# Expert outputs summed into tokens by one-hot matmuls instead of read-add-write transfers, in a hybrid attention and sparse-expert block

## What is computed

```
logits = t @ w_router + b_router
top_val, top_idx = lax.top_k(logits, 4)
gate = softmax(top_val)
# for every expert e, over the tokens that chose it:
gu = xb @ w_gate_up[e] + b_gate_up[e]            # 1024 -> 2048
g, u = min(gu[:, :1024], 7), clip(gu[:, 1024:], -7, 7)
a = (u + 1) * (g * sigmoid(1.702 * g))
yb = a @ w_down[e] + b_down[e]                   # 1024 -> 1024
# x[token] += gate[token, e] * yb[row of that token]
```

## Time and profile before

| | |
|---|---|
| median of 3 runs | 1463.76 us (1462.33 to 1465.62) |
| the profiled execution | 1464.02 us |
| its span, first to last instruction | 1462.0 us |
| PE busy | 1342.6 us, 92% |
| DVE, ACT, POOL busy | 462.0, 270.6, 162.1 us |
| DMA over the span | 458.15 MB, 313 GB/s |
| mean granted PE clock | 0.985 |

### The profile page before, as it was taken

How to read it: one execution, slowest core, us unless ns; L and a number is a source line. 1 busy time by engine, 2 the same in 40 slices (tenths; PEclk the granted TensorE clock), 3 DMA queues, 4 the chain that set the end, 5 groups by cost and what they waited for, 6 DMA issues and landing times.

```text
span 1462.0 us, 26871 instructions
## 1 busy us (share of the span) xinstructions
PE 1342.6 (92%) x10905; PEld 656.5 (45%) x10905; DVE 462.0 (32%) x1112; ACT 270.6 (19%) x476; POOL 162.1 (11%) x247
## 2 busy tenths in 40 slices
PE   6999999999989999989898898989898898989986
PEld 5888878888933333323232232323233233323321
DVE  5113745665263232222222222232222223222211
ACT  4224535542221110011010000101000011110001
POOL 2001300000010111111010111111011111101111
PEclk9999999999999999999999999999999999999998
DMA  6332220013589999999999999999999999999993
GB/s 188 89 113 87 86 87 1 1 32 131 228 321 378 411 411 402 409 409 417 412 405 420 398 415 409 415 412 412 416 402 416 405 415 415 413 414 406 417 403 113
DMA packets 74614, 458.15 MB, mean 313 GB/s; under 512 B 10672, under 2 KB 28112, under 8 KB 41776
## 3 DMA queue, kind: packets, MB, share of 16 engines
q1 hardware_dynamic: 64544, 433.87, 72.9%
q0 software_dynamic: 9344, 21.37, 6.0%
q10 hardware_dynamic: 688, 2.38, 0.4%
HBM read 442.91 MB, written 14.68 MB: 313 GB/s over the span
## 4 chain that ended last, share of the span: by engine, by line
PE 70%; DMA 27%; ACT 1%; DVE 1%; issue 0%; POOL 0%; SPq 0%; ACTq 0%; DVEq 0%; POOLq 0%
PE ps L1659 28%; DMA gu_head<-in_w_gate_up_dram 13%; DMA gu_tail<-in_w_gate_up_dram 13%; PE ps L1698 9%; PE ps L1704 4%; PE ps L1371 3%; PE ps L1373 3%; PE ps L1372 3%; PE ps L1508 2%; PE ps L1395 2%; PE ps L1396 2%; PE ps L1397 2%; PE ps L1686 1%; PE ps L1362 1%; PE ps L1364 1%; PE ps L1363 1%
## 5 line engine op out<-in xcount | busy, mean ns | idle before, releaser
L1659 PE MATMUL ps<-gu_head,xT 128*32 128x512 f32 x3840 | 436.5, 607 | 72.7 <-DMA gu_head<-in_w_gate_up_dram 70.9
L1659 PEld LDWEIGHTS ps<-gu_head,xT 128*32 128x32 f32 x3840 | 122.5, 112 | 379.7 <-issue 271.7
L1186 DVE TENSOR_REDUCE row_f<-ps 128x2 f32<-128x4 f32 (+1 forms) x33 | 5.3, 161 | 513.1 <-PE ps L1623 513.1
L827 ACT COPY gu_tok<-ps 128x512 f32<-128x512 f32 x80 | 46.9, 586 | 607.8 <-PE ps L1659 607.8
L1659 PE MATMUL ps<-gu_tail,xT 128*32 128x512 f32 x1280 | 145.1, 599 | 11.0 <-DMA gu_tail<-in_w_gate_up_dram 11.0
L1698 PE MATMUL ps<-dn_even,aT 128*32 128x512 f32 x1024 | 122.0, 594 | 0.0
L1698 PE MATMUL ps<-dn_odd,aT 128*32 128x512 f32 x1024 | 113.2, 594 | 1.9 <-DVE y_b L1229 1.9
L617 POOL DMA_INDIRECT xg_a<-h_dram,idx_g x33 | 33.2, 1007 | 572.4 <-PE ps L1636 284.1
L880 DVE TENSOR_TENSOR st_l<-st_w,st_h 128x2048 fp32r<-128x2048 f32 x25 | 57.3, 2292 | 112.8 <-ACT st_h L689 112.8
L1659 PEld LDWEIGHTS ps<-gu_tail,xT 128*32 128x32 f32 x1280 | 41.0, 111 | 110.9 <-issue 84.8
L1222 DVE SCALAR_TENSOR_TENSOR aT<-act_u,act_g 128x768 f32<-128x768 f32 (+1 forms) x32 | 26.4, 825 | 158.6 <-PE ps L1704 119.3
(11 more groups left out here) (343 smaller groups left out, 1631.0 us busy)
## 6 DMA issues: line engine op xcount, KB each, us to landing
gu_head<-in_w_gate_up_dram SPq DMA_DIRECT2D x96, 2048.0 KB, 26.2
gu_tail<-in_w_gate_up_dram SPq DMA_DIRECT2D x32, 2048.0 KB, 26.9
dn_even<-in_w_down_dram SPq DMA_DIRECT2D x64, 1024.0 KB, 25.1
dn_odd<-in_w_down_dram SPq DMA_DIRECT2D x64, 1024.0 KB, 25.9
st_w<-in_w_in_dram SPq DMA_DIRECT2D x17, 1024.0 KB, 5.3
st_w<-in_w_out_dram SPq DMA_DIRECT2D x4, 1024.0 KB, 5.2
x_tok<-in_x_dram SPq DMA_DIRECT2D x4, 512.0 KB, 6.0
st_w<-in_w_o_swa_dram SPq DMA_DIRECT2D x4, 512.0 KB, 3.6
```

Of the source, the lines that this page charges most:

```text
L1659: ins = pe.matmul(ps[j * GROUP:(j + 1) * GROUP, n, :], xT[:, k, n * GROUP:(n + 1) * GROUP], gu_chunk(k)[:, j * 512:(j + 1) * 512], start=( ...
```

## The change

The output no longer receives additions by DMA. After `down(i)`, ACT writes the gated result as `y_hi` in fp32r and DVE (`keep_low`) what is missing to full precision as `y_lo`; both are 128 rows of 512: partitions 0 to 63 hold channels 0 to 511 of 64 slots, partitions 64 to 127 the other 512 channels. POOL builds one-hot tables (`put`): row of a slot, column of its token. In `gate_up(2)`, after every second channel block, PE multiplies table by rows (`pair_sums`): for a block `c` of 128 tokens 12 matmuls with 64 rows of contraction each, alternating between the upper and lower half of the array and between PSUM banks 6 and 7. DVE adds each block to the resident `x_tok` (`add_sums`), and PE's next block waits for that. `x_tok` is stored once at the end by SP. The rows gathered by POOL now come whole (one DMA per item, rows of 4 KB) and are turned by DVE in 32x32 blocks (`turn_rows`) and no longer by PE, except for item 0. After the loop, PE's order is down(30), gate_up(31), pair sums, turn_gate_up(31), down(31), sums of item 31.

```diff
-            def gather(small):
-                g.indirect_dma_start(out=xg_a[:, :], out_offset=None, in_=h2_rows[:, :],
-                                     in_offset=bass.IndirectOffsetOnAxis(ap=idx_g[:, 0:1], axis=0)).then_inc(xg_in, 16)
...
+            def gather(i):
+                n = 2 * GROUP if i % 2 else SLOTS
+                g.indirect_dma_start(out=xg[0:n, :], out_offset=None, in_=h2_dram[:, :],
+                                     in_offset=bass.IndirectOffsetOnAxis(ap=idx_g[0:n, 0:1], axis=0)).then_inc(xg_in, 16)
+            def put(table, n):
+                g.tensor_scalar(table[:, :], token_of[:, :], put_row[:, n:n + 1], None, ALU.is_equal).then_inc(put_ready, 1)
...
-                    gather(i % 2 == 1)
-                    add_rows(i - 1, pair)
+                gather(1)
+                pool.wait_ge(sums_ps, pair * 4 + 4)
...
+                put(put_odd, 0)
+                put(put_even, 1)
+                put(put_even_b, 2)
...
+                gather(2)
...
+                for a in (0,) if i % 2 else (0, 1):
+                    ins = sc.activation(y_hi[i % 2 * 2 + a][:, :], ps[:, 4 + a, :], ACT.Identity,
+                                        scale=gate_all[:, col, a:a + 1].rearrange("p a n -> p (a n)"))
+                ins.then_inc(y_high, 1)
...
+            def turn_rows(i, pair=None):
+                rows = slice(0, groups(i) * GROUP)
+                dve.wait_ge(xg_in, counted(32, 16 * i + 16, pair))
+                dve.wait_ge(bank_done, counted(5, groups_before(i), pair))
+                near = xg[:, :].rearrange("s (k p a) -> s p k a", p=P, a=2)
+                for n in range(groups(i)):
+                    s = slice(n * GROUP, (n + 1) * GROUP)
+                    for q in range(4):
+                        r = slice(q * GROUP, (q + 1) * GROUP)
+                        ins = v.transpose(xT[r, :, s].rearrange("r (k a) s -> r k a s", a=2),
+                                          near[s, r].rearrange("s p k a -> s k a p"))
+                ins.then_inc(x_raw, 1)
+                dve.wait_ge(x_raw, counted(2, i + 1, pair))
+                v.tensor_tensor(xT[:, :, rows], xT[:, :, rows], bc(g2_near[:, :], 2, groups(i) * GROUP), ALU.mult).then_inc(xT_ready, 1)
...
+            def keep_low(i, pair=None):
...
+                    ins = v.scalar_tensor_tensor(out=y_lo[n][:, :], in0=ps[:, 4 + a, :],
+                                                 scalar=gate_all[:, col, a:a + 1].rearrange("p a n -> p (a n)"),
+                                                 in1=y_hi[n][:, :].bitcast(F32), op0=ALU.mult, op1=ALU.subtract)
+                ins.then_inc(y_kept, 1)
+            def add_sums(c, n):
+                dve.wait_ge(sums_ps, n)
+                v.tensor_tensor(x_tok[:, c, :], x_tok[:, c, :], ps[:, 6:8, :].rearrange("p h n -> p (h n)"),
+                                ALU.add).then_inc(sums_added, 1)
...
+            def sums(parts, c, pair, n):
+                pe.wait_ge(sums_added, n)
+                for at, (table, y) in enumerate(parts):
+                    for half in (y_hi[y], y_lo[y]):
+                        for h in (0, 1):
+                            rows = slice(h * HD, (h + 1) * HD)
+                            ins = pe.matmul(ps[:, 6 + h, :], table[rows, c * P:(c + 1) * P], half[rows, :],
...
+                    if i == 2 and k % 2:
+                        pair_sums(k // 2, pair)
...
                     lists(i + 2, pair)
-                    turn_rows(i + 1, pair)
                     turn_gate_up(i, pair)
                     down(i - 1, pair)
+            down(0, n_pairs)
             gate_up(1, n_pairs)
+            for c in range(NB):
+                pair_sums(c, n_pairs)
             turn_gate_up(1, n_pairs)
-            down(0, n_pairs)
             down(1, n_pairs)
...
+            for c in range(NB):
+                sums(((put_odd, 2),), c, n_pairs, n_pairs * 4 + (c + 5)).then_inc(sums_ps, 1)
```

More of the change, by code:

```diff
@@ L307, in hybrid_block @@
         pairs_f = r2.put("pairs_f", [1, 1])
[L308 to L314, removed]
+        assert r2.at <= y_end
         r2.rewind(28 * K)
@@ L655, in _ @@
-            gather(False)
-            for c in range(NB):
-                pool.wait_ge(acc_set[c], 16)
+            pool.wait_ge(x_raw, 2)
+            gather(2)
             pool.wait_ge(items_ready, 1)
             n_pairs = pool.value_load(pairs[0:1, 0:1], min_val=PAIRS, max_val=MAX_PAIRS)
-            with pool.Fori(0, n_pairs) as pair:
-                for i in (1, 2):
-                    pool.wait_ge(idx_ready, pair * 2 + (i + 3))
-                    pool.wait_ge(xT_ps, pair * 2 + (i + 2))
-                    pool.sem_inc(turn, 1)
-                    gather(i % 2 == 1)
-                    add_rows(i - 1, pair)
@@ L667, in _ @@
[L667 to L668 removed]
+            pool.wait_ge(bdn_ps, 8)
+            g.memset(y_hi[2][:, :].bitcast(F32), 0.0)
+            then(g.memset(y_lo[2][:, :].bitcast(F32), 0.0))
+            g.tensor_copy(put_odd[:, :], y_lo[2][:, :].bitcast(F32)).then_inc(put_ready, 1)
+            then(g.tensor_copy(put_row[:, 1:3], row_all[:, 0, :]))
+            put(put_even, 1)
+            put(put_even_b, 2)
+            with pool.Fori(0, n_pairs) as pair:
+                pool.wait_ge(idx_ready, pair * 2 + 4)
+                pool.wait_ge(x_raw, pair * 2 + 3)
+                pool.sem_inc(turn, 1)
+                gather(1)
+                pool.wait_ge(sums_ps, pair * 4 + 4)
+                g.tensor_copy(put_row[:, 0:1], row_all[:, bass.ds(pair * 2 + 1, 1), 0:1].rearrange("p a n -> p (a n)"))
+                g.tensor_copy(put_row[:, 1:3], row_all[:, bass.ds(pair * 2 + 2, 1), :].rearrange("p a n -> p (a n)")).then_inc(row_copied, 1)
+                pool.wait_ge(row_copied, pair + 1)
+                pool.sem_inc(turn, 1)
+                put(put_odd, 0)
+                put(put_even, 1)
+                put(put_even_b, 2)
+                pool.wait_ge(idx_ready, pair * 2 + 5)
+                pool.wait_ge(x_raw, pair * 2 + 4)
+                pool.sem_inc(turn, 1)
+                gather(2)
@@ L1325, in _ @@
                     pick(i + 2, later, pair)
+                    if i == 2:
+                        for c in range(NB):
+                            add_sums(c, pair * 4 + (c + 1))
                     index(i + 2, pair)
                     keep_gates(i + 2, pair)
-                    move_rows(i + 1, pair)
+                    turn_rows(i + 1, pair)
                     activate(i, e, pair)
-                    if i == 1:
-                        weigh_odd(0, pair)
+                    keep_low(i - 1, pair)
+            keep_low(0, n_pairs)
+            for c in range(NB):
+                add_sums(c, n_pairs * 4 + (c + 1))
             e = dve.value_load(experts[0:1, bass.ds(n_pairs * 2 + 1, 1)], min_val=0, max_val=E - 1)
             activate(1, e, n_pairs)
-            weigh_odd(0, n_pairs)
+            keep_low(1, n_pairs)
+            for c in range(NB):
+                dve.wait_ge(sums_added, n_pairs * 4 + (c + 2))
+                add_sums(c, n_pairs * 4 + (c + 5))
         @block.tensor
```

216 lines of the change are left out of this document (98 added, 118 removed).

## The result

| | before | after |
|---|---|---|
| median, both kernels on one chip | 1464.3 us | 1483.9 us |
| ratio, 95% interval | 1 | 1.0127 [1.0112, 1.0142] |
| again, as run e1 | 1465.6 us | 1482.3 us, 1.0114 [1.0096, 1.0132] |
| span of the profiled execution | 1462.0 us | 1481.0 us (e1) |

The change makes the kernel 1.1 to 1.3% slower. I had forecast 1454 us, 0.7% faster; the result lies inside my range (1443 to 1492), on the other side of no change.

A forecast was written before the change was run, and what follows sets the result against it. DMA engines were taken to bound the steady state, with PE 12% behind. Start 489, loop 860 and end 103 gave a span of 1452 us, so 1454 against 1463.8, 0.7% faster; range 1443 to 1492.

The forecast's parts named there:

- the 2.6 to 3.6 that I gave: Loop: without the additions' packets, 3.6 us per pass, the DMA bound falls from 64.4 to 60.8 or 61.8 us.
- the price of a block transpose: DVE's turn of gathered rows: taken as 0.36 us per 256 elements, range 0.33 to 0.78; rival of slow transposes, chance 0.23.
- DVE "just in time" at T: Before gate_up(3): DVE's work after T ends at T + 8.3, PE wants to start at T + 8.8.
- I take 0.36: DVE's block transpose of 256 elements taken as 0.36 us each, since only the reading side steps.
- the pass of 61.4: Loop: 61.4 us per pass, from 61.1 for PE and 60.8 to 61.8 for DMA; before, 64.4.
- T + 8.8: When PE wants gate_up(3), after lists, 12 transposes (1.5 us) and down(1) (6.9 us).
- T + 8.5: When DVE is ready for gate_up(3), as the prediction's GpSimd tables rival states its own price.
- the 0.5 that I spoke of: Margin at T before gate_up(3) between DVE's readiness and PE's request: only 0.5 us.
- my own rule of 0.08 per 0.01 above 0.40: Before gate_up(3): from 0.40 us per transpose on, each 0.01 us more costs 0.08 us per pass.
- the rival that I had given 0.07: GpSimd's three tables stop DVE 0.7 us each behind T: pass 63.2 us, time 1479; chance 0.07.
- my 860: Loop: 14 intervals of 61.4 us make 860 us, where before stood 890.3.
- The gather moves the same bytes in one DMA per item and keeps the rest: DMA in the loop: whole-row gathers cost no more than before, so the additions' 3.6 us per pass is gained.

The follow-up runs named there:

- e1: The changed kernel run again unchanged, for a trace of an ordinary execution; 1482.3 us, 1.0114 against the kernel before.
- e3: The kernel before without its DMA additions to the output and the wait for them; 1415.3 us, 0.9662.
- e11: Changed kernel with fourth addition and tables late, PE turning item 1's rows, old tail order, half rows gathered onto 128 partitions, 128-element transposes; 1464.5 us.
- e5: The changed kernel with POOL's three tables built behind the gather of the next rows instead of ahead of it; 1478.4 us, 1.009.
- e4: The changed kernel with DVE's fourth addition of sums behind the activation of item 2 instead of ahead of its list; 1479.1 us, 1.0099.
- e14: e13 with the gather put back to whole rows of 4 KB on 64 or 96 partitions and block transposes of 256 elements; 1446.6 us.
- e13: e11 with DVE's gate operations behind the bias additions, separate PSUM banks in the tail, and y_lo left out of the sums; 1424.1 us.
- e8: The changed kernel with 26 unread matmuls of 512 columns in PE's gap ahead of the first gate_up(1); 1479.5 us, 1.0102.
- e2: The changed kernel with y_lo left out of the sums, 6 instead of 12 matmuls per block; 1469.2 us, 1.0028.

## Why the prediction was wrong

**Right.** Weights bound the kernel before, and the additions cost them about what I said: 2.95 us per pass (e3) against 3.6, inside the 2.6 to 3.6 that I gave. Their waits went. PE became the bound. A block of sums is 1.59 us, and the changes of form cost about 0.1 each. That the whole turned on the price of a block transpose, and at which place, was right as well: PE waits for DVE exactly before `gate_up(3)`, and nowhere else in the loop.

**The step that failed: DVE "just in time" at T, with "I take 0.36", and with it the pass of 61.4.** T, the end of the last block of sums in `gate_up(2)`, is 962.12 in e1. PE would have begun `gate_up(3)` at T + 8.9, and I had T + 8.8. DVE let it begin at T + 9.7, where my terms give T + 8.5 (the T + 8.3 was with 0.34 per transpose). So the margin was 0.3 us and not the 0.5 that I spoke of. Two terms were too small:

- The eight transposes take 3.61 us up to the product instead of 2.88, 0.73 more. A transpose is 0.448 us, because its fixed part is 0.18 us (e11), while I had priced it like an addition. The rule of the Trainium skill that I had weighed for it, 1.73 instead of 1.05 ns per column for a hopping source (Vector Engine (DVE) Microarchitecture Reference, Measured stream behaviour on trn2), doesn't show here: the slope is 1.03 ns per element. By my own rule of 0.08 per 0.01 above 0.40 this alone costs 0.4 us per pass, which isn't enough to turn the sign.
- The list and the gates take 2.04 us instead of 1.4, 0.64 more. This is the rival that I had given 0.07: GpSimd's tables hold up DVE, 0.69 us per pass by e5. A table takes 1.56 us, where I had 0.5 to 0.8, but it doesn't stop DVE for its whole length.

The other terms come out 0.14 below mine and PE 0.10 later: 0.73 + 0.64 - 0.14 - 0.10 - 0.32 of margin is the wait of 0.81. I had priced each rival alone, and the two add up. That the wait was DVE's is shown by e4, which takes it away, and e5, which leaves 0.12 us of it; no run has cheaper transposes, so their part is worked out from rows.

The rule that I had cited for the tables (the Trainium skill, SBUF — State Buffer, SBUF: two separate sides) names a second case beside two SBUF inputs, a DVE operation in a mode that uses two ports. The copy has one SBUF source, takes 0.62 instead of 0.17, and ends at 964.50, just when `put_odd` does (964.47), which agrees with an exclusion; which mode it ran in, no row shows. For a whole instruction the trace doesn't bear the exclusion out: both products of the gates have two SBUF inputs and end inside `put_even` (964.45 to 966.01, as far as POOL's rough times go).

PE's own rows were too small as well. Without the wait a pass takes 61.85 us (e4), where I had 61.1: blocks and the quarters of `gate_up(2)` around them are 0.50 above forecast, since each quarter after a block starts about 0.1 slower, and the two turns of `gate_up`, 1.61 and 1.33 instead of 1.53 and 1.16, 0.25. The wait and what is lost with it make the other 1.01, and the pass 62.86. Over 14 intervals this is 20 us above my 860: 14 from the wait, 6 from the 0.45 between 61.85 and my 61.4.

**"The gather moves the same bytes in one DMA per item and keeps the rest" was wrong too.** It costs all DMA traffic 1.8 us per pass, because the rows land on fewer partitions (63.1 us in e14 against 61.3 in e13). It is not in the result, since PE's 62.86 hid it, but it is why e4 and e5 gained 3 and 4 us only, and it would have taken the forecast's 61.4 up to 63.3 once the lead was used, in a kernel with a perfect DVE.

**The start, 5.6 us over.** The gap ahead of the first `gate_up(1)` grew from 1.88 to 6.11 us: DVE's turn lies in it, with eight transposes at 0.448. From the lists to `gate_up(1)` this is 3.7 us more, where I had added 3. That a gap of this length brings the lower clock, 2.5 us more, I had priced at the tail only (e8). `gate_up(0)` also begins 1.3 us later than before, where I expected it 1 us sooner. Its rows don't land sooner, and PE's gap ahead of them is 3.07 us instead of 2.04. The transposes of these rows and the stretch from there to `gate_up(0)`, first in the kernel before, then in e1:

```profile
426.19 0.74 PE L1633 MATMUL ps<-ident,xg_a 128*128 128x128 f32 x4 [2.04 <-DMA xg_b<-h_dram,idx_g]
426.19:428.89 2.70, 2.70 (x15) 1.61 (x15) 1.26 (x4) 0.00 (x0) 0.00 (x0) 1.00 0.60 185
...
426.37 1.35 PE L1659 MATMUL ps<-ident,xg 96*128 96x96 f32 x8 [3.07 <-DMA xg<-h_dram,idx_g]
426.37:430.21 3.84, 3.61 (x13) 1.87 (x14) 2.31 (x7) 0.00 (x0) 0.00 (x0) 0.60 0.64 226
```

The granted clock is 0.60 instead of 1.00, and that stretch is 1.1 us longer. No run took this gap away, so that it brought the clock down is read from the trace only.

**The end, 3.4 us over.** The largest part is the clock behind the gaps: 12.4 instead of 10.4 us for `down(30)`, and 8.6 instead of 6.9 for `down(31)`. That is 3.7 us, where I had 2 for all. The gap ahead of `down(30)` is 5.0 and not 4, `gate_up(30)` with its sums 27.5 and not 27.0, and the last blocks run at the lower clock.

**The chances.** I gave 0.49 to faster with a margin of 0.3 us at T resting on an operation that no row showed. The honest reading was that any two small surprises there turn the sign.

## What to carry to other kernels

Where a forecast leaves half a microsecond between two engines in each pass, price the lateness with all rivals at once and not one at a time, and move everything behind the handover that the other engine doesn't wait for: an addition, three gate operations and three tables here. Removing work from the engine that bounds the pass is worth only the distance to the next bound, so measure that one before (e2, e3), and let gathered rows land on all 128 partitions. A tail that loses its overlap costs twice, by the gap and by the clock behind it.

## What the hardware showed unexpectedly

- A gather of 0.26 or 0.39 MB onto 64 or 96 partitions pulls the rate of all queues down to 317 to 327 GB/s (e14); weight packets of 16 KB then take about 0.83 us instead of 0.61. Onto 128 partitions the rate stays at 431 GB/s (e13), and at 407 where the third group's rows land on 64.
- Shares of DMA time above 100% do free time when work is taken away: the additions' 3.6 us of engine time gave 2.95 us per pass (e3).
- Beside GpSimd tables of 1.56 us a DVE copy of 128x2 elements takes 0.62 us instead of 0.17 and one product 0.50 instead of 0.22, while two casts, a reduction, a second product of the same form and the block transposes are not touched (e1, e5). A table beside the products of the activation gets longer too, 2.68 us (e5).
- A block transpose of 32 partitions costs 0.18 us and 1.03 ns per element, by two sizes (128 and 256 elements, e11 and e1), with a source that reads every second word.
- Behind gaps of PE of 4 to 6 us PE runs at the lower clock for 3 to 5 us, and it does behind one of 3.07 us at the start; behind one of 2.04 there and the waits of 0.8 us in the loop it doesn't. It does so at the last two of the final four blocks of sums as well, between blocks of four matmuls with gaps of 1.3 us (a first pair takes 0.79 instead of 0.50 us), but not at the blocks of twelve matmuls with the same gaps (0.50).
